# Decode state updates from two partition groups, and two buffers for rotated index heads with later transposes

## The reference, cut to what matters

```python
def rope(x, pos):
    half = x.shape[-1] // 2
    ...
    x1 = x[..., :half].astype(F32)
    x2 = x[..., half:].astype(F32)
    return jnp.concatenate([x1 * cos - x2 * sin, x1 * sin + x2 * cos], axis=-1).astype(x.dtype)

qi = rope(p['idx_q'].reshape(B, L, IDX_H, IDX_D), pos)
ki = rope(p['idx_k'][:, :, None, :], pos)[:, :, 0, :]
```

```python
w_end = jnp.exp(b[..., -1:] - b + igc - m_new[..., None])
decay = jnp.exp(b[..., -1] + m - m_new)
C_new = decay[..., None, None] * C + jnp.einsum('bhs,bhsk,bhsv->bhkv', w_end, kc, vc)
n_new = decay[..., None] * n + jnp.einsum('bhs,bhsk->bhk', w_end, kc)
```

## Time and profile before

| | us |
|---|---|
| median of three executions | 2904.51 |
| the profiled execution, its own time | 2901.19 |
| its span from first to last instruction | 2899.4 |
| PE busy | 2778.3 (96%) |
| DVE busy | 1252.3 (43%) |
| ACT busy | 583.4 (20%) |
| POOL busy | 419.6 (14%) |
| TensorE clock granted, mean | 0.978 |

### The profile page before, as it was taken

The page is one execution under the profiler, slowest core; times in us unless marked ns, Lnnn a source line. Parts: engine busy times, 40 slices in busy tenths (PEclk is TensorE's granted clock), DMA queues, the critical chain, the costliest instruction groups (busy, mean ns, idle before and its releaser), DMA issues. The chain is left out here.

```text
span 2899.4 us, 35783 instructions
## 1 busy us (share of the span) xinstructions
PE 2778.3 (96%) x13681; PEld 1970.7 (68%) x13681; DVE 1252.3 (43%) x2165; ACT 583.4 (20%) x1367; POOL 419.6 (14%) x819
## 2 busy tenths in 40 slices
PE   8987999999999999999999999999699999699998
PEld 6663448874864488888888888888455564455553
DVE  3142388767755644132222144441322330345453
ACT  3121458643000000000000100100222221111211
POOL 0000014212000000000000022220133100333431
PEclk9998989999999999999999999999899999699999
DMA  6447302122122312212342354443844204665652
GB/s 229 93 143 212 127 20 65 47 70 83 48 86 78 111 47 63 81 62 86 104 131 69 94 163 146 140 144 109 307 140 144 88 33 135 210 198 165 200 162 77
DMA packets 272965, 341.25 MB, mean 118 GB/s; under 512 B 40876, under 2 KB 225956, under 8 KB 267516
## 3 DMA queue, kind: packets, MB, share of 16 engines
q1 hardware_dynamic: 235788, 259.50, 28.6%
q0 software_dynamic: 16288, 67.46, 7.5%
q10 hardware_dynamic: 20720, 12.01, 1.4%
HBM read 261.44 MB, written 80.01 MB: 118 GB/s over the span
## 5 line engine op out<-in xcount | busy, mean ns | idle before, releaser
L1341 PE MATMUL sbank<-w,xT 128*128 128x256 f32 x3328 | 728.4, 380 | 2.9 <-ACT w L1373 2.9
L1341 PEld LDWEIGHTS sbank<-w,xT 128*128 128x128 f32 x3328 | 631.9, 190 | 92.6 <-ACT w L1373 3.7
L1341 PE MATMUL sbank<-w,area 128*128 128x256 f32 x1664 | 361.3, 379 | 0.0
L1731 DVE TENSOR_TENSOR pout_b<-pout_b,sbank 128x256 f32<-128x256 f32 x320 | 134.2, 420 | 511.3 <-PE sbank L1341 414.2
L1341 PEld LDWEIGHTS sbank<-w,area 128*128 128x128 f32 x1664 | 316.0, 190 | 42.8
L1689 DVE TENSOR_TENSOR w<-w 128x2048 f32<-128x2048 f32 x64 | 145.1, 2288 | 327.3 <-PE sbank L1341 266.7
L2034 PE MATMUL at_bank_bc<-w,at_hT 128*128 128x512 f32 x512 | 230.0, 593 | 3.9 <-ACT at_bc_out L2189 3.9
L1416 ACT ACTIVATE pout_b<-sbank 128x256 f32<-128x256 f32 x128 | 48.0, 382 | 918.7 <-PE sbank L1341 669.8
L1341 PE MATMUL sbank<-w 128*128 128x256 f32 x832 | 181.7, 379 | 0.0
L1341 PEld LDWEIGHTS sbank<-w 128*128 128x128 f32 x832 | 158.1, 190 | 21.5
L1338 PE MATMUL sbank<-xT,w 128*128 128x512 f32 x384 | 166.6, 593 | 0.0
(11 more groups left out here) (437 smaller groups left out, 3346.4 us busy)
## 6 DMA issues: line engine op xcount, KB each, us to landing
w<-in_w_in SPq DMA_DIRECT2D x64, 1024.0 KB, 5.2
proj<-pout_b SPq DMA_DIRECT2D x208, 128.0 KB, 1.7
area<-in_x_prompt SPq DMA_DIRECT2D x16, 1024.0 KB, 5.1
attention_then_units<-proj SPq DMA_DIRECT2D x128, 128.0 KB, 2.8
area<-roped_q_of_decode POOLq DMA_DIRECT2D x32, 256.0 KB
w<-in_w_out SPq DMA_DIRECT2D x4, 2048.0 KB, 15.9
y_of_groups_b_c<-at_bc_out SPq DMA_DIRECT2D x32, 256.0 KB
out_sample_C<-mo_dec_states SPq DMA_DIRECT2D x32, 256.0 KB, 3.5
```

What stands on the lines that cost most here:

```text
L1341: last = nc.tensor.matmul(bank[t][:, 0:256], x(c, t * P, (t + 1) * P), at[name][:, c, :], start=first_ and c == 0, stop=c == 7, skip_group ...
L1731: nc.vector.tensor_tensor(out[:, t, :], x[:, t, :], product_at(n, t), ALU.add).then_inc(sums_read, 1)
```

## The change

Three things change in the first stage. `rix` has a second buffer (it lies on a table of the gates that is no longer read by then), so that DVE waits for the transposes and the key store of tile `n - 2`; the key store has two semaphores. And the table of the transposes is another.

In the last stage `dk1`, `dkw`, `dv` and `dec_row_of` lie on 64 partitions. Partitions 0 to 31 hold the first 128 key dimensions of each head, 32 to 63 the second 128, and the values are there twice. The two matmuls of a decode state take their rows from partitions 0 to 31 and from 32 to 63. That needs one more load of keys by SP ahead of the stage, two more DMAs of ACT at its start, and one more small matmul for the gate columns on partitions 32 to 63. POOL's operations have 64 partitions by 128 elements where they had 32 by 256.

```diff
@@ project_index
-        rix = part((IDX_H + 1) * IDX_D, "p (h d) -> p h d", d=IDX_D)
+        rixs = [part((IDX_H + 1) * IDX_D, "p (h d) -> p h d", d=IDX_D),
+                area[:, 6 * TOK:6 * TOK + (IDX_H + 1) * IDX_D].rearrange("p (h d) -> p h d", d=IDX_D)]
...
-            return {i + 4: {10: 0}, i + 5: {4: 1, 10: 2}, i + 6: {4: 3, 10: 4}, i + 7: {10: 5}, v: {2: 6, 9: 7}, v + 1: {4: 8}
-                    }.get(m, {})
+            return {i + 5: {4: 0, 14: 1}, i + 6: {8: 2, 15: 3}, i + 7: {8: 4}, i + 8: {0: 5}, v: {2: 6, 7: 7, 12: 8}}.get(m, {})
...
-                nc.gpsimd.dma_start(outs[f"{who}_kidx"][dst, :], rix[0:r, IDX_H, :]).then_inc(kidx_stored, 16)
+                nc.gpsimd.dma_start(outs[f"{who}_kidx"][dst, :], rixs[n % 2][0:r, IDX_H, :]
+                                    ).then_inc(kidx_stored[n % 2], 16)
...
-                if n:
-                    dve.wait_ge(g_turned, 2 * n)
-                    dve.wait_ge(kidx_stored, 16 * n)
-                rotate_products(nc.vector, order, r, ix[0:r, u], cs2[0:r, u], rix, tb, IDX_H + 1, IDX_D // 2)
+                if n >= 2:
+                    dve.wait_ge(g_turned, 2 * n - 2)
+                    dve.wait_ge(kidx_stored[u], 16 * (n // 2))
+                rotate_products(nc.vector, order, r, ix[0:r, u], cs2[0:r, u], rixs[u], tb, IDX_H + 1, IDX_D // 2)
@@ attend_bc, SP, ahead of the last stage
+                    sp.dma_start(k.area[NS:2 * NS, 8192 + ML_W:8192 + 2 * ML_W].rearrange("t (h c n) -> t h c n", h=ML_H, c=2)[:, :, 0, :],
+                                 k.proj[SEQ:TOK, C_K:C_K + ML_W].rearrange("t (h c n) -> t h c n", h=ML_H, c=2)[:, :, 1, :]
+                                 ).then_inc(k.dqk_in, 16)
@@ mix_out
-        dq1, dk1 = T("dec_q_slot", [P, 2, ML_H, 2, NS]), T("dec_k_slot", [NS, 2, ML_D])
-        dv, dkw = T("dec_v", [NS, ML_H, V1]), T("dec_kw", [NS, ML_W])
+        dq1, dk1 = T("dec_q_slot", [P, 2, ML_H, 2, NS]), T("dec_k_slot", [2 * NS, 2, P])
+        dv, dkw = T("dec_v", [2 * NS, ML_H, V1]), T("dec_kw", [2 * NS, ML_H, P])
...
-            act.dma_start(drow[:, :], ins["dec_row_of"][:, :]).then_inc(consts_in, 16)
-            act.dma_start(dv[:, :, 0:ML_D], k.proj[SEQ:TOK, C_V:C_V + ML_W].rearrange("t (h d) -> t h d", h=ML_H)
-                         ).then_inc(dv_in, 16)
+            for x in range(2):
+                act.dma_start(drow[NS * x:NS * (x + 1), :], ins["dec_row_of"][:, :]).then_inc(consts_in, 16)
+                act.dma_start(dv[NS * x:NS * (x + 1), :, 0:ML_D],
+                             k.proj[SEQ:TOK, C_V:C_V + ML_W].rearrange("t (h d) -> t h d", h=ML_H)).then_inc(dv_in, 16)
...
-                        nc.gpsimd.tensor_scalar(dkw[:, h * ML_D:(h + 1) * ML_D], dk[:, h * ML_D:(h + 1) * ML_D],
-                                                cols[0:NS, NCH, 2, h:h + 1], None, ALU.mult).then_inc(d_kw, 1)
+                        nc.gpsimd.tensor_scalar(dkw[:, h, :], dk_of[:, h, 0, :], cols[0:2 * NS, NCH, 2, h:h + 1], None,
+                                                ALU.mult).then_inc(d_kw, 1)
...
-                    nc.gpsimd.tensor_tensor(dk1[:, m % 2, :], dkw[:, h * ML_D:(h + 1) * ML_D],
-                                            drow[:, b:b + 1].to_broadcast([NS, ML_D]), ALU.mult).then_inc(k_slot, 1)
+                    nc.gpsimd.tensor_tensor(dk1[:, m % 2, :], dkw[:, h, :], drow[:, b:b + 1].to_broadcast([2 * NS, P]),
+                                            ALU.mult).then_inc(k_slot, 1)
...
                 for c in range(2):
-                    last = nc.tensor.matmul(kv[c][:, 0:V1], dk1[:, u, c * P:(c + 1) * P], dv[:, h, :], start=True,
-                                            stop=True)
+                    half = slice(NS * c, NS * (c + 1))
+                    last = nc.tensor.matmul(kv[c][:, 0:V1], dk1[half, u, :], dv[half, h, :], start=True, stop=True)
...
+            last = nc.tensor.matmul(acc1[NS:2 * NS, 12 * NCH:12 * NCH + 12], r12[:, SEQ:TOK], k.ident[0:12, 0:12],
+                                    start=True, stop=True)
```

34 lines of the change are left out of this document (18 added, 16 removed).

## The result

The changed kernel takes 2869.26 us in the median of four runs (2866.49 to 2875.06), beside 2904.62 us before: 35.4 us less, a ratio of 0.9888 with a 95% interval from 0.9875 to 0.9900. The profiled execution took 2867.35 us, its span 2865.6. I had forecast 2881.5 and a range that began at 2874.0. The sign and the places were right and the size was too small: 22.8 us forecast, 35.4 measured.

What follows compares the result with a forecast made beforehand. PE, busy 96% of the span, was taken to bound the kernel. First stage 9.3, decode matmuls 13.2 and last stage's start 0.3 sum to 22.8 us off 2904.5: 2881.7, said as 2881.5, range 2874 to 2891 (8 in 10).

Steps and rivals of the forecast that it cites:

- Transposes of tiles 0 to 5: First stage up to tile 6's transposes: waits 8.6, low clock 1.7 and moved transposes 0.6 us go, sum 10.9.
- the walk: First stage, PE's and DVE's lists: no transpose up to tile 5 finds PE early; tile 5's rotation ends 1.5 us ahead.
- The four waits: First stage, PE idle for DVE ahead of transposes: 2.70, 2.67, 1.68 and 1.52 us, 8.6 in all, would go.
- the prediction's own sign: First stage: the mechanism is wrong if a transpose of tiles 0 to 5 has a bracket of over 1 us.
- a chain: First stage, end of tile i + 7 to tile 6's transposes: copy, store, load, rotation, 7.4 us, not shortened.
- a new wait of 1.6 us: First stage, PE ahead of tile 8's transposes, waiting for ACT's copy of tile 7: 1.6 us lost, bounds 0 and 5.
- 1.7 us for a low clock that I expect behind tile 6 as before: First stage, PE behind tile 6's transposes: a low clock adds 1.7 us to its way to tile 8's.
- Decode matmuls: Last stage: two row groups save 0.40 us per decode state, 13.2 us in all, bounds 0 and 14.5.
- The rate read off L1256: Matmuls alternating between two 64-row groups: 0.235 us from start to start against 0.44, so two groups nearly halve the time.
- half and no overlap: Last stage, decode matmuls: row groups overlap by one pass only, 2887.8 us (chance 0.08), or not at all, 2894.9 (0.06).
- a cost per change: Last stage: changing row groups costs about 0.2 us each time, 19 us lost, 2914 us in all; chance 0.03.
- First states and the start: Last stage: start gains 0.3 us net; first decode state saves nothing, second and fourth 0.8 each at the low clock.

Runs made afterwards that it cites:

- e1: The kernel before with the first stage's edit alone (two buffers for rotated heads, the new table): 2890.33 us, ratio 0.9961.
- e3: The changed kernel with both matmuls of a decode state reading partitions 0 to 31, the second half of each key left out: 2888.25 us, ratio 0.9954.
- e7: The changed kernel with the copies of dec_row_of counted on a semaphore of their own: 2867.43 us, ratio 0.9891.
- e9: The changed kernel as it is, measured again beside the kernel before: 2871.22 us, ratio 0.9901.
- e11: The changed kernel with dec_row_of on its own semaphore and VectorE's products L2701 moved ahead of the second scaled_q: 2868.69 us, ratio 0.9895.
- e14: The changed kernel with dec_row_of and the causal mask each on its own semaphore, the start waiting for the mask alone: 2873.34 us, ratio 0.9900.
- e15: The changed kernel as it is, measured once more beside the kernel before: 2872.91 us, ratio 0.9904.
- e16: A repeat of the changed kernel with dec_row_of on its own semaphore: 2875.20 us, ratio 0.9907.
- e4: The changed kernel with the gather of key pages issued one tile earlier, behind the rotation of tile 6: 2880.51 us, ratio 0.9930.
- e12: The kernel before, run once more for a second profile, one execution: 2905.35 us.
- e6: The kernel before with the new table but one buffer for rotated heads, and the old last stage: 2901.82 us, ratio 1.0009.
- e10: The changed kernel with dec_row_of on its own semaphore and the gather behind tile 8's rotation: 2873.18 us, ratio 0.9914.
- e2: The kernel before with the last stage's edit alone: 2887.41 us, ratio 0.9944.

## Why the prediction was wrong in size

**Transposes of tiles 0 to 5: the gain right, 1 us short; the walk wrong for tile 5.** The four waits went, and so did the low clock between them. From 135.46 to the last multiplication of 296 columns (213.76) are 78.3 us before, from 132.17 to 198.45 are 66.3 after: 12.0 instead of 10.9. Some 0.2 us per wait were missing in my sum: from 135.46 the 148 passes at 0.249 (the rate of the later groups) end at 172.3, and the next row stood at 175.20, 2.9 us later, where the bracket says 2.70. Here a bracket is some 0.2 us shorter than what the wait costs: the row of the 148 passes lasts 37.04 us, 0.2 more than 148 times 0.249, because the whole length of the last pass is counted in.

The walk through the lists had tile 5's rotation end 1.5 us ahead of PE. It ended 1.0 us behind PE's arrival (198.86), and by the prediction's own sign, a bracket of over 1 us, this part failed: the bracket is 1.01 to 1.40 us in six of the nine profiles with this stage and this gather (the changed kernel, `e1`, `e3`, `e7`, `e9`, `e11`, `e14`, `e15`, `e16`) and 0.38 to 0.89 in the others. It cost nothing that shows, because PE had next to wait for tile 6 in any case. `e14` has another, 1.91 us ahead of tile 3, where VectorE stood 8.61 us for the load. The buffer isn't what the waits before had in common: of the four, only tile 2's hung on the key store (4.00 us on VectorE); tile 0's came from the gates' work, and those of tiles 4 and 5 hung on their loads (5.53 and 7.84 us), like tile 6's.

**From tile 6 to the stage's end: this step failed.** The prediction took over from the profile before the 12.4 us between tile 6's transposes and ScalarE's copy of tile 7's heads, and made of it "a new wait of 1.6 us" ahead of tile 8. In the changed kernel's profile these 12.4 us are 6.1, and there is no wait. PE reached tile 8's transposes 10.2 us behind tile 6's; with 0.75 us for the copy, it waits only if the 12.4 are above 9.5. In the nine profiles they are 6.1 to 12.1, with a median of 8.8, and only `e15` (1.78 us) and `e14` (2.93) have the wait. What changed is how long tile 6's stores take: from the second store's issue to ScalarE's next copy 4.2 to 10.2 us (median 6.9), against 9.7 to 11.7 in the three profiles of the old stage. I had named "if the stores land ahead of it, the wait is nil" and used it only as an end of the range. It does not explain the rest: in the other eight the stores landed behind the gather's issue and six of these have no wait, and the gather goes out behind these stores in both kernels, by 3.3 to 5.0 us in the nine and by 3.8 to 4.4 in the three. Why they land sooner in the new order stays open. `e4` shows only the price of a gather ahead of them.

"1.7 us for a low clock that I expect behind tile 6 as before" failed too: the granted clock is 1.00 from 205.5 to 215.7, and of the nine only `e14` has a low clock ahead of the stage's last matmul, behind its wait for tile 8. The bracket ahead of tile 6, forecast near 3 us, is 0.65: the transposes of tile 5 (0.6), PE's wait for them (1.13) and a chain shorter by 0.7 came out of the 3.20. That chain, from the last multiplication to tile 6's transposes (213.76 to 221.48 before, 198.45 to 205.48 after), I had left unchanged; it is 6.8 to 7.3 us in eight of the nine and 7.7 to 8.2 in the three before. The gap ahead of the second stage was 0.7 us shorter in this profile, and that is luck: it was 8.2 to 9.6 us in six of the nine, where ScalarE, held by tile 7's stores until after PE's last matmul, came late to the memory banks.

The stage by terms: 9.3 forecast + 1.1 (above) + 1.6 (wait) + 1.5 (low clock) + 0.7 (chain) + 0.7 (gap) = 14.9; the other 3.3 of the profile's 18.1 lie ahead of the change, the low clock at 102 above all. By the medians the stage gains 15.2. My upper bound for it, 12.5, moved two terms only and was too low.

**Between the stages: forecast 0, 2.4 in the profile.** Chance: the stretch takes 2211.0 and 2215.9 us in `e9` and `e15`, and 2214.3 in `e12`.

**Decode matmuls: right.** 0.40 us forecast, 0.43 measured. The 27 steps from the fifth state on take 307.7 and 296.4 us: 11.3 less. The rate read off L1256 held, full overlap; `e3` excludes every other source. The rivals of half and no overlap and of a cost per change are out. The passes start at 0, 7, 321 and 327 ns, in pairs, so the passes of the two halves alternate. The rule in the Trainium skill (TensorE: Matmul & The Clock Gate, Part 3) that matmuls start and end strictly in program order is not contradicted by that, if both passes are counted as one matmul; what failed was only my reading of it, that the two passes of one matmul must stand next to each other.

**First states and the start.** I gave 0.3 us for the start and 2.0 for the first four states; the profile gives 1.7 for both together (at the fifth state +67.65 before, +65.98 after). The start had the right terms and one missing: GpSimd began 2.0 us later in this pair of profiles (I had up to 1.0; the medians of six profiles with the old start and seven with the new are 8.4 and 9.5, so 1.0 stands), -1.3 for `dkw` (right), and +2.6 for L2701, which no term covered. It cost nothing, since the load of `gate_rows` sets the second state.

The stage's total, 13.3 us beside 13.5 forecast, agrees partly by luck: by the medians it is 15.6. In `e9` and `e15` the last stage is 5 us shorter still. There the clock is at its full level from the second state on (`e9`) or falls once (`e15`), where before it was low for much of this time (0.71 in the mean). From the second state's L3041 to that of the fifth, busy times, clock and DMA share, of before and of `e9`:

```profile
2508.70:2538.00 29.30, 25.48 (x77) 17.55 (x77) 13.58 (x45) 5.24 (x16) 9.78 (x19) 0.71 0.56 171
```

```profile
2493.10:2515.00 21.90, 16.43 (x79) 10.79 (x78) 13.19 (x46) 5.31 (x17) 9.76 (x21) 1.00 0.81 242
```

Whether the shorter matmuls make that likelier isn't settled: three of eleven profiles with the new last stage have no low clock there and two a single spell, and all seven with four passes in a row have two or more, but nothing here moves the clock alone.

**Sum of the error.** 12.6 us = 3.1 (the failed step: the wait 1.6, the low clock 1.5) + 0.7 (the chain to tile 6) + 1.1 (the first waits' size) + 0.7 (the gap) + 3.3 (ahead of the change) + 2.4 (between the stages) - 0.2 (last stage) + 1.5 (median against profile). The gap, the 3.3, the 2.4 and the 1.5 are a lucky draw of the first runs: 7.9 us. Without it the gain would be 27.5, beside which stand 30.6 and 28.4 us in the later measurements; the medians put the difference mostly in the last stage (15.6 us, where this profile has 13.3).

## What to carry to other kernels

Two resources that are each needed for a gain (a buffer and the slot in the order) show nothing alone; ask of each wait what comes second, and don't judge one edit by a run without the other. When an edit moves stores in time, take no store's duration over from one old profile, even where the large transfer behind it keeps its place; and ask what a change of their order would do. Where a row names an engine that had ended its work well before the wait ended, look in the kernel for the other semaphores of that wait. Where waits vary from profile to profile, sum a bound over all terms, not over those that seem open, and widen it by what two profiles of one kernel differ by.

## What the hardware showed

- Two 32-row matmuls on different row groups: four passes of 257 columns in 0.63 us up to the next row, against 1.06 on one group (`e3`).
- VectorE's four products L2701 (two operands, 128 partitions) took 0.45, 1.40, 1.31 and 0.43 us in the changed kernel, and within 0.02 us of that in nine more profiles, beside GpSimd's `tensor_tensor` and its two DMA issues; they took 0.32 to 0.33, 0.21, 0.21 and 0.21 in the six profiles with the old start, beside GpSimd's 32-partition `tensor_scalar`. In the changed kernel the second one ended within 0.1 us of the end of GpSimd's last product. Moved to another place (`e11`), the four took 1.52 us. In `e14` they took 0.68, 1.02, 0.21 and 0.21 beside GpSimd's 64-partition `tensor_scalar`, so the longer times don't need a `tensor_tensor` there. That a faster product on one of these engines lengthens one on the other is what I infer; no run changes GpSimd's work alone.
- The stores of a tile's heads, tiles 0 to 5: landed 2.1 to 6.6 us after their issue (`e6`, `e10`, `e12`, whose profiles show the landings). Tile 6's, with the gather issued 3.3 to 5.0 us behind them: 4.2 to 11.7 us from the second store to ScalarE's next copy (the changed kernel's profile and `e2`'s). Tile 7's, issued behind the gather: 14.9 to 20.5 us in the nine profiles, from the first store on; tile 6's in `e4`, also behind it: 18.4. It isn't the gather alone: `e10`'s 11.3 us had it 7.3 us behind.
